# A gate projection in two pieces per tile inside the stick-breaking attention, and the hand-back of attention tiles on other banks and at other units

## The reference, cut to what matters

```python
proj = h @ w_in
(q_r, k_r, v_r, g_r, q_s, k_s, v_s, g_s, q_f, k_f, v_f, g_f, f_logit) = jnp.split(proj, splits, axis=-1)
logf_new = jax.nn.log_sigmoid((f_logit + b_f).astype(F32))
# stick-breaking, 5 heads of 64: z = q k^T / 8; A = sigmoid(z) * prod over the later keys of (1 - sigmoid(z))
# forgetting, 5 heads: logits q k^T / 8 + C_t - C_s, C = cumsum(logf); softmax
o = jnp.concatenate([o_r * silu(g_r), o_s * silu(g_s), o_f * silu(g_f)], axis=-1)
return (o @ w_out, s_new, ks_new, vs_new, kf_new, vf_new, logf_new)
```

## Time and profile before

| | us |
|---|---|
| median of 3 runs | 3652.8 (3651.75 to 3658.95) |
| the profiled execution | 3648.39 |
| its span, first to last instruction | 3646.8 |
| PE busy | 3214.1 (88%) |
| DVE, ACT, POOL busy | 1311.8, 948.8, 761.4 |
| PE matmuls of L819, all projections | 1485.2 |

### The profile page before, as it was taken

How to read it: one execution, slowest core, us unless ns; L and a number is a source line. 1 busy time by engine, 2 the same in 40 slices (tenths; PEclk the granted TensorE clock), 3 DMA queues, 4 the chain that set the end, 5 groups by cost and what they waited for, 6 DMA issues and landing times. The chain is left out here.

```text
span 3646.8 us, 67770 instructions
## 1 busy us (share of the span) xinstructions
PE 3214.1 (88%) x25256; PEld 1993.1 (55%) x25256; DVE 1311.8 (36%) x2842; ACT 948.8 (26%) x1746; POOL 761.4 (21%) x1250
## 2 busy tenths in 40 slices
PE   6999998888999688799989998978889986887998
PEld 4566654555666455444455666645557654554443
DVE  3235075443324444211241350744423244442221
ACT  2012144332225233111021122434322242331110
POOL 0000063544010154300000001724420102452000
PEclk9999989999989798899989999989989888998999
DMA  5011104986120598610121011058841206895102
GB/s 176 19 36 33 49 11 131 306 271 218 33 72 1 149 306 282 221 57 10 46 97 32 26 44 45 1 183 293 288 160 39 67 1 188 290 306 180 55 29 72
DMA packets 268656, 439.67 MB, mean 121 GB/s; under 512 B 48817, under 2 KB 216402, under 8 KB 268338
## 3 DMA queue, kind: packets, MB, share of 16 engines
q1 hardware_dynamic: 205810, 239.96, 20.7%
q0 software_dynamic: 55744, 189.25, 15.8%
q10 hardware_dynamic: 6912, 7.87, 0.6%
HBM read 410.28 MB, written 26.65 MB: 120 GB/s over the span
## 5 line engine op out<-in xcount | busy, mean ns | idle before, releaser
L819 PE MATMUL ps<-W,xT 128*128 128x320 f32 (+7 forms) x5120 | 1485.2, 465 | 11.5 <-DVEq L451 11.5
L819 PEld LDWEIGHTS ps<-W,xT 128*128 128x128 f32 (+1 forms) x5120 | 858.1, 184 | 586.0 <-issue 292.5
L701 POOL DMA_DIRECT2D branch<-in_cache_fox_v_dram x480 | 258.9, 539 | 620.0 <-issue 578.3
L701 POOL DMA_DIRECT2D branch<-in_cache_sb_v_dram x480 | 258.4, 538 | 363.6 <-issue 322.9
L1485 ACT ACTIVATE branch<-ps 128x512 f32<-128x512 f32 x288 | 165.7, 595 | 387.7 <-PE ps L1065 379.2
L1065 PE MATMUL ps<-C,W 128*128 128x128 f32 x1280 | 199.0, 300 | 74.5 <-DMA W<-in_cache_fox_k_dram 27.6
L959 PE MATMUL ps<-branch 64*128 64x512 f32 (+7 forms) x480 | 220.4, 589 | 39.1 <-POOLq L451 20.0
L1065 PE MATMUL ps<-C,branch 128*128 128x128 f32 x1280 | 194.3, 294 | 62.1 <-DMA branch<-in_cache_fox_k_dram 17.1
L1150 PE MATMUL ps<-branch 128*8 128x64 f32 x9920 | 183.5, 235 | 56.5 <-DMA branch<-in_cache_fox_v_dram 29.5
L1065 PEld LDWEIGHTS ps<-C,W 128*128 128x128 f32 x1280 | 150.2, 150 | 142.2 <-issue 65.5
L1087 PE MATMUL ps<-branch,work 128*32 128x512 f32 x896 | 226.1, 619 | 0.7
(11 more groups left out here) (246 smaller groups left out, 3495.4 us busy)
## 6 DMA issues: line engine op xcount, KB each, us to landing
branch<-in_cache_sb_v_dram POOLq DMA_DIRECT2D x480, 160.0 KB, 4.3
branch<-in_cache_fox_v_dram POOLq DMA_DIRECT2D x480, 160.0 KB, 4.1
W<-in_cache_sb_k_dram SPq DMA_DIRECT2D x248, 160.0 KB, 3.4
W<-in_cache_fox_k_dram SPq DMA_DIRECT2D x248, 160.0 KB, 3.6
branch<-in_cache_sb_k_dram SPq DMA_DIRECT2D x240, 160.0 KB, 4.4
branch<-in_cache_fox_k_dram SPq DMA_DIRECT2D x240, 160.0 KB, 4.2
W<-in_w_in_dram SPq DMA_DIRECT2D x14, 1280.0 KB, 6.3
W<-in_w_in_dram SPq DMA_DIRECT2D x9, 1536.0 KB, 7.2
```

The source lines that it names most:

```text
L701: pool.dma_start(ringV[:, g % 2, p * DA:(p + 1) * DA], cache[L, bass.ds(pg, 1)].rearrange("a s h d -> s (a h d)"))\
L819: ins = pe.matmul(out, src[:, k, t * P:t * P + R], W[i % 2][:, k, a:z], start=(k == 0), stop=(k == kc - 1), **place)
```

## The change

`fg` leaves PROJ_F and is computed in ATT_S. Tile k < 8 is cut in two pieces of 4 inner steps, after `turn` of units (k, 0) and (k, 1), and the sample tile follows `turn` of unit (7, 4). Its result lies in bank 7. ACT's sigmoid comes after its copy at h = 1, DVE's gate product after its step at h = 3. Since bank 7 is taken, the output of every attention tile, of both kinds, now lies in bank 6 alone, and is transposed back into bank 7. For that, `copy_out` moves from h = 1 to h = 0, `back` from h = 2 to h = 4 in the stick-breaking kind and to h = 3 in the forgetting kind, `finish` from h = 3 to h = 4 in the stick-breaking kind and stays at h = 3 in the other. The weights change buffers (`fq` and `fv` in `W[0]`, `fk` in `W[1]`). `fq` is loaded at the end of ATT_S, `fk` at the start of PROJ_F, and `out0` when `fv` is done. Exp and Ln of the logits come at the start of `fq`, and the cumulative sums come after `fq` instead of before it.

```diff
+W_OF = {seg: (0 if seg in ("fq", "fv") else 1 if seg == "fk" else i % 2) for i, seg in enumerate(ALL_SEGS)}
-    return 3 + 4 * (n % 2) if seg in IN_RET else n % 3
+    return 3 + 4 * (n % 2) if seg in IN_RET else 7 if seg == "fg" else n % 3
+ATT_FILL = {}
+for _k in range(TILES):
+    _at = [(_k, 0), (_k, 1)] if _k < SAMPLE else [(_k - 1, 4)]
+    _cut = [0, KC // 2, KC] if _k < SAMPLE else [0, KC]
+    for _p, (_a, _z) in enumerate(zip(_cut, _cut[1:])):
+        ATT_FILL[_at[_p]] = (_k, _a, _z)
...
-        PROJ_SEGS = {PROJ_R: SEG_NAMES[0:4], PROJ_S: SEG_NAMES[6:8], PROJ_F: SEG_NAMES[8:12]}
+        PROJ_SEGS = {PROJ_R: SEG_NAMES[0:4], PROJ_S: SEG_NAMES[6:8], PROJ_F: SEG_NAMES[9:12]}
...
# SP
                 load_k(L, kind, 0, 0)
+                if kind == "sb":
+                    load_weights(L, "fq")
                 sp.wait_ge(phase_sem, 4 * ((ATT_S if kind == "sb" else ATT_F) + 1))
...
                 sp.wait_ge(phase_sem, 4 * (DEC_S + 1))
-                load_weights(L, "fq")
+                load_weights(L, "fk")
                 load_decoded(L, "sb")
-                for seg in ALL_SEGS[10:13]:
+                for seg in ALL_SEGS[11:13]:
                     load_weights(L, seg)
...
# PE: segment_tile is cut into its waits and its steps
             def segment_tile(seg, t, L):
+                segment_start(seg, t, L)
+                segment_steps(seg, t, 0, PLE // P if seg[:2] == "pe" else KC)
...
-                    if seg == "fg":
+                    if seg == "fq":
                         pe.wait_ge(logf_ready, 1)
...
# PE: attention, weigh
-                    if c == 0 and i >= 2:
-                        pe.wait_ge(att_done[kind], i - 1)
+                    if c == 0 and i >= 1:
+                        pe.wait_ge(att_copied[kind], i)
...
# PE: attention, back
-                    pe.wait_ge(att_copied[kind], NT - t)
+                    i = NT - 1 - t
+                    pe.wait_ge(att_copied[kind], i + 1)
+                    if i >= 1:
+                        pe.wait_ge(att_done[kind], i)
+                    if kind == "sb":
+                        pe.wait_ge(emptied_dve, evac_count("fg", i + 1))
...
# PE: attention, the loop
-                    if h == 2 and i >= 1:
+                    if h == (4 if kind == "sb" else 3) and i >= 1:
                         back(t + 1)
                     turn(u)
+                    if kind == "sb" and (i, h) in ATT_FILL:
+                        k, first, end = ATT_FILL[i, h]
+                        if first == 0:
+                            done = i if k == SAMPLE else i - 1
+                            if done >= 1:
+                                pe.wait_ge(att_done[kind], done)
+                            segment_start("fg", k, L)
+                        segment_steps("fg", k, first, end)
...
# ACT: attention, the loop
                     to_sbuf(u)
-                    if h == 1 and i >= 1:
+                    if h == 0 and i >= 1:
                         copy_out(t + 1)
+                    if kind == "sb" and h == 1:
+                        gate_tile("fg", i)
+                if kind == "sb":
+                    gate_tile("fg", SAMPLE)
                 copy_out(0)
...
# DVE: projection
+                        if seg == "fq" and t == 2:
+                            dve.wait_ge(logf_act, 2)
+                            dve.scalar_tensor_tensor(logf, logit, 0.0, ltmp, ALU.min, ALU.subtract)\
+                                .then_inc(logf_ready, 1)
...
# DVE: attention, the loop
                     (stick if kind == "sb" else largest)(u)
-                    if h == 3 and i >= 1:
+                    if kind == "sb" and h == 3:
+                        gate_tile("fg", i)
+                    if h == (4 if kind == "sb" else 3) and i >= 1:
                         finish(t + 1)
                     if kind == "fox" and h == 4 and 1 <= i <= 2:
                         page_sums(L, i - 1)
+                if kind == "sb":
+                    gate_tile("fg", SAMPLE)
                 finish(0)
```

More of the change, by code:

```diff
@@ L89, in bank_of, with same_buffer, loads_of @@
     n = ALL_SEGS.index(seg) * TILES + t
-    return 3 + 4 * (n % 2) if seg in IN_RET else n % 3
+    return 3 + 4 * (n % 2) if seg in IN_RET else 7 if seg == "fg" else n % 3
+def same_buffer(seg):
+    return [s for s in ALL_SEGS[:ALL_SEGS.index(seg)] if W_OF[s] == W_OF[seg]]
+def loads_of(seg):
+    return 1 + sum(s != "rq" for s in same_buffer(seg))
+ATT_FILL = {}
[4 more added lines that the diff above has]
+        ATT_FILL[_at[_p]] = (_k, _a, _z)
 def seg_width(seg):
@@ L299, in step_program @@
         squares = cut(work, 2200, HA, HD)
-        logit = cut(work, 2600, TILES, HA)
+        logit = sb("logit", [P, TILES, HA])[:]
         ltmp = cut(work, 2650, TILES, HA)
@@ L503, in load_weights @@
             def load_weights(L, seg):
-                i = ALL_SEGS.index(seg)
-                if i >= 2:
-                    sp.wait_ge(proj_ready, TILES * (i - 1))
+                users = same_buffer(seg)
+                if users:
+                    sp.wait_ge(proj_ready, TILES * (ALL_SEGS.index(users[-1]) + 1))
                 if seg in SEG_COL:
@@ L515, in load_weights @@
                     kc = PLE // P if seg[:2] == "pe" else KC
[L516 to L517 removed]
+                sp.dma_start(W[W_OF[seg]][:, 0:kc, 0:n], src.rearrange("(k p) n -> p k n", p=P))\
+                    .then_inc(w_loaded[W_OF[seg]], 16)
             def load_k(L, kind, b, g, pages_of_group=PG8):
@@ L794, in segment_tile, with segment_start @@
             def segment_tile(seg, t, L):
+                segment_start(seg, t, L)
+                segment_steps(seg, t, 0, PLE // P if seg[:2] == "pe" else KC)
+            def segment_start(seg, t, L):
                 i = ALL_SEGS.index(seg)
                 n = i * TILES + t
-                R, N = rows(t), SEG_W.get(seg, 512)
                 if t == 0 and seg == "rq":
@@ L808, in segment_tile @@
                     pe.wait_ge(norm_out, (TILES if seg == "pg0" else 0) + t + 1)
-                back = 2 if seg in IN_RET else 3
+                back = 2 if seg in IN_RET else 1 if seg == "fg" else 3
                 if n >= back:
@@ L813, in segment_tile, with segment_steps @@
                     pe.wait_ge(emptied_dve if s3 in DVE_EVACUATES else emptied_act, evac_count(s3, t3))
+            def segment_steps(seg, t, first, end):
+                R = rows(t)
                 src = pT if seg[:2] == "pe" else xT
                 kc = PLE // P if seg[:2] == "pe" else KC
-                for k in range(kc):
+                for k in range(first, end):
                     for out, a, z in pieces(seg, t):
                         place = dict(tile_position=(0, ROWS if a else 0), skip_group_check=True) if t == SAMPLE else {}
-                        ins = pe.matmul(out, src[:, k, t * P:t * P + R], W[i % 2][:, k, a:z],
+                        ins = pe.matmul(out, src[:, k, t * P:t * P + R], W[W_OF[seg]][:, k, a:z],
                                         start=(k == 0), stop=(k == kc - 1), **place)
-                ins.then_inc(proj_ready, 1)
+                if end == kc:
+                    ins.then_inc(proj_ready, 1)
             def turn_tile(seg, t):
@@ L943, in retention, with attention @@
                 phase_over(pe, RET)
-            def attention(phase):
+            def attention(phase, L):
                 kind = KIND[phase]
@@ L1224, in _ @@
                 phase_over(pe, PROJ_S)
-                attention(ATT_S)
+                attention(ATT_S, L)
                 decode(DEC_S, L)
@@ L1228, in _ @@
                 phase_over(pe, PROJ_F)
-                attention(ATT_F)
+                attention(ATT_F, L)
                 decode(DEC_F, L)
@@ L1311, in project @@
                     i = ALL_SEGS.index(seg)
+                    if seg == "fq":
+                        act.wait_ge(logit_ready, 1)
+                        act.activation(ltmp, ltmp, ACT.Exp).then_inc(logf_act, 1)
+                        act.wait_ge(logf_act, 1)
+                        act.activation(ltmp, ltmp, ACT.Ln, bias=1.0).then_inc(logf_act, 1)
                     for t in range(TILES):
@@ L1376, in project @@
                         turned_to(seg, TILES - 1)
[L1377 to L1382, removed]
             def retention():
@@ L1444, in copy_out @@
                         act.wait_ge(att_back[kind], NT - 1 - t)
-                    act.activation(att_oT[kind][:, 0:2 * P], ps[:, 6 + t % 2, 0:2 * P], ACT.Copy)
-                    act.activation(att_oT[kind][0:HD, 2 * P:3 * P], ps[0:HD, 6 + t % 2, 2 * P:3 * P], ACT.Copy)\
+                    act.activation(att_oT[kind][:, 0:2 * P], ps[:, 6, 0:2 * P], ACT.Copy)
+                    act.activation(att_oT[kind][0:HD, 2 * P:3 * P], ps[0:HD, 6, 2 * P:3 * P], ACT.Copy)\
                         .then_inc(att_copied[kind], 1)
@@ L1617, in project @@
                     i = ALL_SEGS.index(seg)
-                    if seg == "fg":
```

(6 more changed lines are left out.)

12 lines of the change are left out of this document (4 added, 8 removed).

## The result

| | median (lowest to highest) | span of the profiled execution |
|---|---|---|
| before, 9 runs | 3651.75 (3638.00 to 3661.26) | 3646.8 |
| after, 9 runs | 3670.32 (3660.82 to 3676.99) | 3668.8 |

The account below looks back on a forecast made before the run. PE, busy for 88% of the span, was taken as the bound. The terms -88.0 + 70.6 + 22.2 + 8 + 1 gave +13.8 us, so 3666 us, range 3640 to 3686.

Parts of the forecast that it names:

- A: PROJ_F: taking `fg` out, with the stall before the sums, saves 44.0 us a layer, 88.0 us in all.
- B: ATT_S: the `fg` matmuls placed there cost 35.3 us a layer, 70.6 us in all, bounds 64 and 77.
- C: ATT_F: later `back` lengthens PE's wait before scores(i + 1, 1); with `copy_out` 11.1 us a layer, 22.2 in all.
- D: ATT_F: lengthened waits make the clock fall more often, six further falls possible at 45% each; 8 us, bounds 0 and 18.
- third rival: ATT_F: every lengthened wait drops the clock, 18 us instead of 8; +23.8 us, 3677 us; chance 15%.
- E: Loads: `fq` before DEC_S's key pages at nothing, `out0` beside the last v store 0.5 us a layer; together 1 us.

Follow-up runs that it names:

- r2: The changed kernel, unedited, profiled once more; one run, 3681.03 us.
- e1: Changed kernel with `back` again at h = 2 in the forgetting kind (ATT_F); 3628.09 us, ratio to before 0.9933.
- e2: Changed kernel with `finish` moved behind DVE's step of h = 4 in the forgetting kind, `back` left at h = 3; 3604.85 us, 0.9873 of before.
- e3: Changed kernel with `fq` loaded behind the last loads of DEC_S instead of at the end of ATT_S; 3668.02 us, 1.0045 of before.
- e4: Changed kernel with `out0` loaded after ATT_F has begun instead of at the end of `fv`; 3658.54 us, 1.002 of before.
- e7: Changed kernel with the first `fg` tile whole behind turn(0, 1) instead of in two pieces behind turn(0, 0) and turn(0, 1); one run, 3665.46 us.
- e8: Changed kernel with `back` at h = 2 in the forgetting kind and `out0` loaded after ATT_F has begun; 3620.62 us, 0.9913 of before.
- e9: Changed kernel, forgetting kind with `back` at h = 2, `copy_out` at h = 1, `finish` behind h = 4; `out0` loaded after ATT_F has begun; 3592.48 us, 0.984 of before.
- r1: The kernel before, unedited, profiled once more; one run, 3655.58 us.
- e6: Kernel before with only the attention hand-back changed (bank 6 alone, `back` into bank 7, moved units); `fg` stays in PROJ_F; 3694.21 us, 1.0102 of before.
- e10: Changed kernel with `fq` loaded only after DEC_S is over, no weights loaded under the decode; one run, 3670.34 us.
- second pair: One more profile of either kernel, before at 3655.58 us and changed at 3681.03 us.

## Why the prediction was right, and where by luck

*A, right, 7 us too small.* Idle time before the sums gone, `fq` first. The sums ran 0.9 and 1.9 us faster. The other 4.3 us are the slow start of PROJ_F in the first profile of before, clock 0.72 and 0.56 over the first 6 us. I had said that it passes to `fq`; it did not, the clock was 1.00 there in both layers of after, r2, e1 to e4 and e7 to e9. But r1, the same kernel as before, also has 1.00 in both layers, and against it A is 90.8 us. So these 4.3 us are in part or whole the luck of one execution, and not the work of the change. When the phase starts slow is not shown: e6, whose PROJ_F is that of before, has 1.00 in one layer and 0.58 in the other, and e10, where PE had waited 7.3 and 7.5 us for `fq`, has 0.52 and 0.65.

*B, mis-sized, and the step that failed.* "If the clock rises at the same moment as before" was wrong. It rose 10 to 11 us earlier, and the tile at i = 0, priced at 4.4 us, made its stretch 1.0 us shorter in the first layer and 0.4 in the second: 5.4 of the 6.6 and 4.8 of the 5.8 us by which B was too dear there. ATT_S grew by 28.7 and 29.5 us, under the 31 at which I had called myself wrong. From i = 1 to 6 the piece of work was priced rightly (3.4 to 4.4 us a tile).

*C, right in mechanism and size.* Waits of 2.9 us at i = 1, DVE idle for over 4.5, and idle time +20.0 against 22.2 us. e1 removes it at PE, e2 at DVE, and e6 brings it by the hand-back alone.

*D, right in kind, too small.* 14.9 us in the first profile and 20.9 in the second, against 8 with bounds 0 and 18. Over the seven profiles with `back` and `finish` where the change put them it was 13.7 to 21.5, 16.9 on average. The third rival described ATT_F better than the forecast. I had given each new fall of the clock 45%; in both profiles and both layers a fall began within 2 us of the end of every wait at i = 1 to 5, waits of 2.9 to 2.4 us. In both layers of r2 and of e6 the mean clock of the phase was 0.75, for 0.83 and 0.81 before. The Trainium skill (page "TensorE: Matmul & The Clock Gate", section "HAM oscillation — how this bites in real kernels") tells of such a fall once per tile in a kernel that waits some 3 to 5 us between tiles. Here the shorter waits of 2.4 to 2.9 us were enough each time, and before the change waits of about 1 us were enough at some tiles.

*E, mis-sized: 1 us against 19.5 (16.3 in the second pair).* ATT_F's first wait grew by 3.4 and 4.0 us, above my bound of 3 a layer; e4 took 2.9 and 3.1 of it back, so this part is shown. DEC_S grew by 12.2 us in the two layers together (9.0 in the second pair), above my bound of 2 a layer; some 2 x 3.3 of it may go to the load of `fq`, with the reserve stated above. I had asked only whether the first key pages come in time, which they did (first matmul on them 11.1 us into the phase, before 10.9), and not what 1.3 MB do to the pages behind them.

*What I had not considered:* 6 us ahead of the first ATT_S, in instructions that the change does not touch. From 240 to 360 us into the span PE was busy throughout in both kernels, and the clock was lower after (before, then after):

```profile
240.00:300.00 60.00, 60.00 (x298) 40.32 (x297) 32.43 (x67) 7.33 (x16) 3.86 (x7) 0.98 0.06 20
300.00:360.00 60.00, 60.00 (x326) 42.21 (x325) 34.35 (x77) 17.37 (x27) 5.03 (x7) 0.94 0.15 42
```

```profile
240.00:300.00 60.00, 60.00 (x278) 38.95 (x277) 30.58 (x61) 6.47 (x14) 3.85 (x7) 0.90 0.06 20
300.00:360.00 60.00, 60.00 (x321) 42.10 (x319) 33.33 (x74) 15.37 (x24) 5.01 (x7) 0.90 0.15 42
```

Both pairs of profiles agree on it, e6 and most other kernels are like after, and e7 is near before (457.3 us). It lies in RET, which took 135.9 us before and 142.9 after. In the second layer, where the two kernels run the same RET again, it took 138.4 and 136.0 us in the profiles of before and 138.4 in both of after, and up to 141.8 in the other kernels. So RET varies without any edit, and how much of the 6 us the change makes is open, and so is the cause.

The forecast thus came near the number with A and B 19 us too dear together, D, E and this clock 31 us too cheap, and C and the rest 4 us too dear.

## What to carry to other kernels

When an evacuation or a hand-back is moved, look at what stands behind its wait on the waiting engine: put it after the step on which the bottleneck's next work hangs (here one condition on DVE was worth 65 us by the medians of after and e2), and not merely near its producer. Do not price a load at nothing because the first page of the phase still comes in time (here the decode took some 3 us more a layer with 1.3 MB under it, likely by the load), and keep a large load from running beside a store that a phase boundary waits for. Dense matmuls put into a stretch at the slow clock can cost less than nothing, so price them at either clock and not only at that of before.

## What the runs showed of the hardware

The clock rose 4.5 to 5.9 us after `turn(0, 0)` with eight 325-column matmuls behind it, and only after 14.8 to 16.3 us in the same unit order without them, though PE was busy throughout in both. In ATT_F of the changed kernel the clock was at 0.50 for the 4 us that followed a wait of 2.88 us, and again at 1.00 from 1126:

```profile
1114.00:1118.00 4.00, 1.12 (x5) 0.63 (x4) 3.79 (x9) 1.90 (x3) 0.00 (x0) 0.88 0.01 2
1118.00:1122.00 4.00, 4.00 (x22) 2.56 (x22) 2.75 (x5) 1.00 (x3) 0.00 (x0) 0.50 0.00 0
1122.00:1126.00 4.00, 4.00 (x27) 2.86 (x24) 0.12 (x1) 1.41 (x2) 0.00 (x0) 0.76 0.01 4
1126.00:1130.00 4.00, 4.00 (x30) 3.25 (x28) 1.45 (x4) 2.03 (x6) 0.00 (x0) 1.00 0.00 0
```

In its two profiles, both layers, each of the waits of 2.9 to 2.4 us at i = 1 to 5 was met by such a fall.

One 80 KB store took 5.7 us to land beside a 2 MB load (both profiles) and 2.3 and 2.4 us without it.
